# Block 2 attention: probabilities turned by VectorE and DMA instead of TensorE

## The chip, the core and the metric

The kernel runs on one core of one Trainium2 chip. The metric is device time in microseconds (us), the median over several executions. The engines are TensorE (PE; PEld is its weight load), VectorE (DVE), ScalarE (ACT), GpSimd (POOL) and SyncE (SP), whose queue issues nearly all DMAs.

## The reference, cut to what matters

Two blocks follow each other on a sequence of 512 rows of width 1024, in float32. Block 1 (windowed attention, a convolution, a gated feed-forward net) is not touched. Block 2 has two layers; each has 8 heads of chunked attention with a relative bias and 4 heads of retention. The part that the change touches is this attention:

```
scores = jnp.einsum("bnqhd,bnkhd->bnhqk", qc, kb) * (dh ** -0.5)
...
bias = rel_bias.astype(jnp.float32)[:, jnp.clip(dist, -REL_CLIP, REL_CLIP) + REL_CLIP]
...
scores = jnp.where(valid, scores + bias[None, None], NEG_INF)
p = jax.nn.softmax(scores, axis=-1)
out = jnp.einsum("bnhqk,bnkhd->bnqhd", p, vb)
...
y = jnp.concatenate([ya * jax.nn.silu(ag.astype(jnp.float32)),
                     yr * jax.nn.silu(rg.astype(jnp.float32))], axis=-1).astype(x.dtype)
return x + y @ w_out.astype(x.dtype)
```

A query in chunk c (64 rows) sees all keys of chunks 0 to c, its own chunk whole. The query rows are handled in four tiles i = 0 to 3 of 128 rows, and tile i needs 128(i+1) keys.

## The kernel before, in words

Each engine has its own queue, written out by hand in program order (class `Queues`, lines 174 to 217). An instruction waits for the names in its list and holds up whatever stands behind it on the same engine. `take` and `free` (303 to 310) guard buffers: who takes one waits for whoever freed it. Float32 products are made of a high and a low part: ScalarE rounds a tile to float32r (`wh` for weights), another engine subtracts to get the low part (`wl`), and TensorE does three matmuls (`mm3`), or two where one operand holds both parts. `prepare_to` (361) readies the weights three units ahead; the `wl` goes to GpSimd for the units in `POOL_LOW` (85), to VectorE for the rest. Each `wl` also releases the DMA of a later weight unit on SP.

Block 2 runs per layer through 26 steps, one for each entry of `SLOTS` (81): a projection of 24 matmuls of 512 columns, then `pieces_after` (1561), which puts the pieces of the attention between the projections. Each head's four query tiles come as two halves, tiles (3, 0) and (2, 1), 640 columns each, one half per step in steps 0 to 15. A half goes through this pipeline:

- Step s, `half_scores`: TensorE writes the scores into banks 4 and 5. `half_soft` (1402): VectorE adds the bias from the table tile `HK` and takes the row's extreme in one instruction (`m`, line 1417), does the same for the last 64 columns of the lower 64 rows (`M`, line 1421; the upper 64 rows of those columns hold a mask filled once by the loop at 1232), ScalarE takes the exponential with its row sum (`e`), VectorE the reciprocal of the sum (`r`, line 294), GpSimd multiplies the probabilities by it (`pn`, line 290), and a DMA copies the 640 columns to the tile `UA` (`pm`).
- Step s+2, `half_turn` (1447): TensorE turns the five 128x128 squares into banks 6 and 7 (line 249). `half_split` (1460): ScalarE rounds them to the high part (`ph`), VectorE subtracts (`pl`).
- Step s+3, for the second half, `head_values` (1479): 8 matmuls of values and turned probabilities into bank 3. `head_finish` (1499): ScalarE and VectorE add the two halves of the bank (`both_halves`, 877), GpSimd multiplies by the gate (`yg`), and the result is split for the output projection (`yh`, `yl`).

Within a step, TensorE's order is projection, values, turns, scores. Steps 16 to 25 hold the retention heads; they turn no probabilities, but their statistics go through small transposes on TensorE (`turn_squares`, `spread`) with a chain of short VectorE instructions (`head_rstd`, 530) between the two.

Of the kernel before, what the change touches and what calls it, by code (L numbers as in the profile page):

```python
# [28 lines left out]
MASKED = -1e30  # L29
# [20 lines left out]
XBH, XBL = Z + 22528, Z + 26624  # L50
PR = Z + 26368
R_COLS = Z + 30720


TP, TI = 0, 1280
T_COLS = TI + 128
# [13 lines left out]
TG0, TG1 = COS, Y + 5632  # L70
F_COLS = Y + 6760
X0H, X0L = Z + 16896, Z + 20992
# [11 lines left out]

POOL_LOW = {f"{l}{u}" for l in range(2) for u in ("q0", "v7", "k5", "q6", "q7", "k7", "g5", "g6", "g7")}

# [133 lines left out]
def two_blocks_kernel(nc, w_units, consts, dmat, x, x_rows, pvec, positions, rel, gain, out, stop=None):  # L220
# [6 lines left out]
    with ctx:  # L227
        RA = ctx.enter_context(nc.sbuf_tensor("RA", [128, R_COLS], F32R))
        FA = ctx.enter_context(nc.sbuf_tensor("FA", [128, F_COLS], F32))
        UA = ctx.enter_context(nc.sbuf_tensor("UA", [128, T_COLS], F32R))  # L230
        PS = [ctx.enter_context(nc.psum_tensor(f"ps{i}", [128, 512], F32)) for i in range(8)]
        Q = Queues()
# [998 lines left out]

        for i in range(4):
            G(f"fill.{i}", ["acl.21", "sin"], lambda e, i=i: e.memset(  # L1233
                F(SB + hoff[i] + 128 * i + 64, 64, 0, 64), -MASKED))

        zero("z2", K2P, 2048, ["gemm.br7"])

        for l in range(2):
# [89 lines left out]
            def evac_qk(i, w, b, key):  # L1328
# [73 lines left out]
            def half_soft(h, half):  # L1402
                pair = ((3, 0), (2, 1))[half]
                for n, i in enumerate(pair):
                    b = 4 + n
                    w = 128 * (i + 1)
                    pc = PB + hoff[i]
                    if h >= 8:
                        V(f"{pre}pn.{h}.{i}", [f"{pre}s.{h}.{i}", f"{pre}D.{h}"] + take(f"pb{i}"),
                          mul(F(pc, w), bank(b, w), F(DT + 512 * (h % 2), w)))  # L1410
                        free(f"bank{b}", f"{pre}pn.{h}.{i}")
                        continue
                    sc = SB + hoff[i]
# [6 lines left out]
                    V(f"{pre}M.{h}.{i}", [f"{pre}m.{h}.{i}"],  # L1420
                      lambda e, sc=sc, w=w, b=b, hk=hk, i=i: e.tensor_tensor_reduce(  # L1421
                          F(sc + w - 64, 64, 64, 128), bank(b, 64, w - 64, 64, 128),
                          steps(F(hk - w + 64, 1, 64, 128), [[-1, 64]]), -1.0, F(NM + i, 1, 64, 128),
                          ALU.add, ALU.min, F(NM + i, 1, 64, 128)))
                    free(f"bank{b}", f"{pre}M.{h}.{i}")
                    A(f"{pre}e.{h}.{i}", [f"{pre}M.{h}.{i}"] + take(f"pb{i}"), func(
                        F(pc, w), F(sc, w), ACT.Exp, scale=-1.0, bias=nm, accum=F(DE + i, 1)))
                    free(f"sb{i}", f"{pre}e.{h}.{i}")
                yield
                if h < 8:  # L1430
                    for i in pair:
                        V(f"{pre}r.{h}.{i}", [f"{pre}e.{h}.{i}"], recip(F(RD2 + i, 1), F(DE + i, 1)))
                    for i in pair:
                        w = 128 * (i + 1)
                        pc = PB + hoff[i]
# [3 lines left out]
                    for i in pair:  # L1439
                        free(f"pb{i}", f"{pre}pm.{h}.{half}")  # L1440
                if half == 1:
                    last = f"{pre}pn.{h}.1" if h >= 8 else f"{pre}M.{h}.1"
                    free(f"{'hk' if h < 8 else 'dt'}{h % 2}", last)
                    if h + 2 < 12:
                        load_head(h + 2)

            def half_turn(h, half):

                for n, i in enumerate(((3, 0), (2, 1))[half]):
                    if h >= 8:  # L1450
                        continue
                    b = 6 + n
                    for j in range(i + 1):
                        after = [f"{pre}pm.{h}.{half}"] + take(f"bank{b}") if j == 0 else []
                        T(f"{pre}pT.{h}.{i}" if j == i else None, after,
                          turn(bank(b, 128, 128 * j), U(TP + hoff[i] + 128 * j, 128)))
                if h < 8:
                    free(f"tp{half}", f"{pre}pT.{h}.{(0, 1)[half]}")

            def half_split(h, half):  # L1460
                parts = []
                for n, i in enumerate(((3, 0), (2, 1))[half]):
                    w = 128 * (i + 1)
                    if h < 8:
                        b = 6 + n
                        src = bank(b, w).rearrange("p (j q) -> p j q", j=i + 1)
                        d = lambda c, i=i: steps(R(c + 128 * i, 128), [[384, i + 1], [1, 128]])
                        parts.append((i, src, d(P2H), d(P2L), f"{pre}pT.{h}.{i}", f"bank{b}"))
# [30 lines left out]
            def head_finish(h):  # L1499
                if h < 8:  # L1500
                    yield from both_halves(f"{pre}yr.{h}", [f"{pre}o.{h}"] + (take("acc") if h % 2 == 0 else []), h % 2, ACC)
                    if h % 2:
                        p = h // 2
                        t, tn = t_slot()
                        G(f"{pre}yg.{p}", [f"{pre}yr.{h}", f"{pre}yr.{h - 1}", f"{pre}gt.{p}"] + take(tn),
                          mul(F(t), F(ACC), F(SG + 512 * (p % 2))))
                        free(f"sg{p % 2}", f"{pre}yg.{p}")
                        free("acc", f"{pre}yg.{p}")

                        def split():  # L1510
                            A(f"{pre}yh.{p}", [f"{pre}yg.{p}"], copy(R(YAH + 512 * p), F(t)))
                            G(f"{pre}yl.{p}", [f"{pre}yh.{p}"], sub(R(YAL + 512 * p), F(t), Rf(YAH + 512 * p)))
                            free(tn, f"{pre}yl.{p}")

                        later.append(split)
# [153 lines left out]
            xtm = [COS, SB, HK, DT]  # L1669
            xfree = [["1k7.l"], ["1e.7.1"], ["1M.7.1"], ["1pn.11.1"]]  # L1670

# [222 lines left out]
```

How the kernel before makes its waits and increments, by code:

```python
    def emit(self, engine, e, sems):  # L208
        waited = {}
        for name, waits, fn, sem, step in self.q[engine]:
            for s, v in waits:
                if waited.get(s, 0) < v:
                    e.wait_ge(sems[s], v)
                    waited[s] = v
            inst = fn(e)
            if name is not None:
                inst.then_inc(sems[sem], step)
# [343 lines left out]
                @block.sync  # L561
                def _(e):
                    Q.emit("sync", e, sems)
                    for s in sorted(Q.count):
                        if s.startswith("out") or stop:
                            e.wait_ge(sems[s], Q.count[s])
```

## Time and profile before

| | |
|---|---|
| median of 3 executions | 1206.74 us (1206.34 to 1206.87) |
| profiled execution, its own time | 1206.78 us |
| its span, first to last instruction | 1205.0 us |
| PE busy | 1196.4 us (99%) |
| DVE busy | 821.9 us (68%) |
| ACT busy | 553.9 us (46%) |
| POOL busy | 377.8 us (31%) |
| granted TensorE clock, mean | 0.998 of full speed |
| attention steps of layer 0 and of layer 1 | 705 to 820 us and 972 to 1087 us of the span |

Busy times come from one execution that the hardware profiler recorded. A matmul's recorded duration overlaps with its neighbours', so TensorE's cost is read from the distance between starts, or from the chain of work that ended last, where each piece counts once. Instructions that a helper issues bear the helper's line: 249 is every TensorE transpose of this kind, 297 every matmul, 274 every two-operand VectorE or GpSimd operation, 266 every ScalarE copy.

### The profile page before, as it was taken

To read this page: it belongs to the slowest core of one execution; us is meant where nothing else is said; L and a number is where in the kernel's file an instruction comes from. 1 tells how busy PE (TensorE), PEld (TensorE's weight loads), DVE (VectorE), ACT (ScalarE), POOL (GpSimd) and SP (SyncE) were. 2 spreads that over 40 slices of the span, in tenths; PEclk is the share of its full clock that TensorE was granted. 3 is DMA by queue.
4 is the path that set the end of the run, shared out by engine and by line. 5 is a ranking of instruction groups with operands and counts; after the bars stand their busy time and mean duration, and the time that the engine had idled before them with its cause. 6 is when DMAs were issued, how large, how long until landed. Compare 5 with 4: busy or idle time off the path is not lost.

```text
span 1205.0 us, 15117 instructions
## 1 busy us (share of the span) xinstructions
PE 1196.4 (99%) x5822; PEld 1008.1 (84%) x5822; DVE 821.9 (68%) x1530; ACT 553.9 (46%) x954; POOL 377.8 (31%) x277
## 2 busy tenths in 40 slices
PE   9999999999999999999999999999999999999997
PEld 7888888888888888888888889898888889898886
DVE  5878735466888536663568777777866866777875
ACT  6567533324444324332434465654334556654433
POOL 0135289997000000000000228775303033375200
PEclk9999999999999999999999999999999999999999
DMA  8233232323323322333223334433223334342251
GB/s 301 76 122 140 105 115 88 105 73 103 105 88 106 105 88 88 105 105 98 80 81 109 122 119 143 149 132 99 79 70 90 120 129 140 134 141 87 87 142 70
DMA packets 46744, 133.68 MB, mean 111 GB/s; under 512 B 4688, under 2 KB 10320, under 8 KB 46672
## 3 DMA queue, kind: packets, MB, share of 16 engines
q1 hardware_dynamic: 46240, 132.27, 33.8%
q8 instruction: 46, 0.75, 0.2%
q10 hardware_dynamic: 432, 0.44, 0.1%
q14 instruction: 26, 0.21, 0.1%
HBM read 114.35 MB, written 2.10 MB: 97 GB/s over the span
## 4 chain that ended last, share of the span: by engine, by line
PE 95%; DVE 2%; POOL 1%; ACT 1%; DMA 0%; issue 0%; ACTq 0%; POOLq 0%
PE ps L297 93%; PE ps L249 2%; DVE RA L274 1%; POOL FA L290 1%; DMA RA<-FA 0%; PE ps L551 0%; PE ps L492 0%; DVE FA L286 0%; ACT RA L266 0%; DVE FA L813 0%; DVE FA L274 0%; ACT FA L271 0%; ACT FA L270 0%; POOL RA L555 0%; DVE FA L1770 0%
## 5 line engine op out<-in xcount | busy, mean ns | idle before, releaser
L297 PE MATMUL ps<-RA 128*128 128x512 f32 (+1 forms) x5470 | 1177.8, 376 | 1.6 <-POOL RA L555 1.3
L297 PEld LDWEIGHTS ps<-RA 128*128 128x128 f32 x5470 | 974.5, 189 | 182.6 <-POOL RA L555 1.3
L266 ACT ACTIVATE RA<-FA 128x1024 fp32r<-128x1024 f32 (+5 forms) x338 | 280.2, 855 | 333.8 <-PE ps L297 167.2
L274 DVE TENSOR_TENSOR RA<-FA,RA 128x1024 fp32r<-128x1024 f32 (+6 forms) x303 | 321.8, 1073 | 162.8 <-ACT RA L266 161.1
L290 POOL TENSOR_SCALAR FA<-FA 128x256 f32<-128x256 f32 (+3 forms) x117 | 147.2, 1271 | 159.9 <-DVE FA L294 158.7
L286 DVE SCALAR_TENSOR_TENSOR FA<-ps,FA 128x512 f32<-128x512 f32 (+4 forms) x161 | 102.1, 638 | 90.8 <-PE ps L297 44.5
L274 POOL TENSOR_TENSOR FA<-FA 128x512 f32<-128x512 f32 (+1 forms) x82 | 108.3, 1322 | 88.1 <-ACT FA L270 66.7
L274 POOL TENSOR_TENSOR RA<-FA,RA 128x512 fp32r<-128x512 f32 (+1 forms) x37 | 69.7, 1893 | 109.5 <-ACT RA L266 109.5
L1233 POOL MEMSET FA<- 64x64 f32 x4 | 0.4, 145 | 328.7 <-ACT RA L266 328.7
L271 ACT ACTIVATE FA<-FA 128x512 f32<-128x512 f32 (+4 forms) x108 | 59.9, 555 | 90.3 <-DVE FA L1421 76.0
L270 ACT ACTIVATE FA<-ps,FA 128x512 f32<-128x512 f32 x56 | 38.1, 684 | 108.3 <-PE ps L297 108.3
L286 DVE SCALAR_TENSOR_TENSOR FA<-FA 128x512 f32<-128x512 f32 (+4 forms) x115 | 65.5, 578 | 16.3 <-ACT FA L266 8.0
L270 ACT ACTIVATE FA<-FA 128x512 f32<-128x512 f32 (+2 forms) x79 | 45.2, 576 | 64.9 <-DVE FA L286 45.0
L274 DVE TENSOR_TENSOR RA<-ps,RA 128x256 fp32r<-128x256 f32 (+3 forms) x109 | 53.4, 528 | 18.1 <-ACT RA L270 15.7
L274 DVE TENSOR_TENSOR FA<-ps,FA 128x512 f32<-128x512 f32 (+3 forms) x96 | 57.6, 619 | 5.8 <-PE ps L297 4.4
L286 DVE SCALAR_TENSOR_TENSOR RA<-FA,RA 128x512 fp32r<-128x512 f32 (+1 forms) x44 | 41.1, 941 | 19.8 <-ACT RA L270 19.0
L274 DVE TENSOR_TENSOR FA<-FA 128x512 f32<-128x512 f32 (+3 forms) x94 | 46.8, 499 | 6.6 <-ACT FA L270 4.0
L291 POOL TENSOR_SCALAR FA<-FA 128x512 f32<-128x512 f32 (+1 forms) x26 | 47.8, 1839 | 2.2
L270 ACT ACTIVATE RA<-FA 128x512 fp32r<-128x512 f32 (+1 forms) x50 | 35.0, 703 | 7.6 <-DVE FA L274 5.6
L266 ACT ACTIVATE RA<-ps 128x256 fp32r<-128x256 f32 (+2 forms) x95 | 37.3, 448 | 0.7
L270 ACT ACTIVATE FA<-ps 64x512 f32<-64x512 f32 (+1 forms) x48 | 28.3, 590 | 12.9 <-PE ps L297 12.0
L274 DVE TENSOR_TENSOR FA<-FA,ps 64x512 f32<-64x512 f32 (+1 forms) x32 | 21.8, 682 | 10.7 <-ACT FA L270 9.7
(51 smaller groups left out, 300.6 us busy)
## 6 DMA issues: line engine op xcount, KB each, us to landing
FA<-w_units SPq DMA_DIRECT2D x188, 512.0 KB, 3.5
UA<-FA SPq DMA_DIRECT2D x32, 320.0 KB, 2.5
RA<-FA SPq DMA_DIRECT2D x10, 512.0 KB, 3.2
FA<-rel SPq DMA_DIRECT2D x16, 256.0 KB, 3.7
FA<-w_units SPq DMA_DIRECT2D x8, 384.0 KB, 3.0
FA<-x SPq DMA_DIRECT2D x8, 256.0 KB, 6.0
FA<-x_rows SPq DMA_DIRECT2D x4, 512.0 KB, 9.4
FA<-dmat SPq DMA_DIRECT2D x8, 256.0 KB, 2.8
```

The costliest lines, as they stand in the source:

```text
L249: return lambda e: e.transpose(dst.bitcast(F32R), src, U(TI, 128))
L266: return lambda eng: eng.activation(dst, src, ACT.Copy)
L270: return lambda eng: eng.activation(dst, src, f, bias=bias, scale=scale)
L271: return lambda eng: eng.activation(dst, src, f, bias=bias, scale=scale, accum_out=accum)
L274: return lambda eng: eng.tensor_tensor(dst, a, b, op)
L286: return lambda eng: eng.scalar_tensor_tensor(dst, a, s, b, op0=op0, op1=op1)
L290: return lambda e: e.tensor_scalar(dst, src, s1, None, op0=op0)
L291: return lambda e: e.tensor_scalar(dst, src, s1, s2, op0=op0, op1=op1)
L297: return lambda e: e.matmul(dst, a, b, start=start, stop=stop_)
L1233: G(f"fill.{i}", ["acl.21", "sin"], lambda e, i=i: e.memset(F(SB + hoff[i] + 128 * i + 64, 64, 0, 64), -MASKED))
```

## The change

The reciprocal of the sum is no longer applied to the probabilities, but to the attention's output: the four reciprocals of a head go to HBM (`rs`), come back spread over 64 partitions (`rl`, into the tile `DB`), and GpSimd multiplies the gated output by them. The mask moves into the bias table: two memsets fill its upper left 64x64 corner once, the table is loaded by two DMAs for each head, and `m` covers all columns, so `M` goes. The probabilities are turned by one VectorE transpose in 32x32 squares (`vt`, into the tile `VT`), four DMAs that write its four groups of 32 partitions to HBM (`st`), and one DMA, issued a step later, that reads the turned half back (`ld`, into the tile `TPF`). `half_split` reads that tile in place of banks 6 and 7. `POOL_LOW` keeps two units per layer of nine; the low parts of rotated queries move from GpSimd to VectorE; in a step, `pl` comes behind the new half's `m` and `e`.

```diff
-POOL_LOW = {f"{l}{u}" for l in range(2) for u in ("q0", "v7", "k5", "q6", "q7", "k7", "g5", "g6", "g7")}
+POOL_LOW = {f"{l}{u}" for l in range(2) for u in ("g5", "g6")}
...
-        for i in range(4):
-            G(f"fill.{i}", ["acl.21", "sin"], lambda e, i=i: e.memset(
-                F(SB + hoff[i] + 128 * i + 64, 64, 0, 64), -MASKED))
+        for i in range(2):
+            G(f"fill.{i}", ["acl.21", "sin"], lambda e, i=i: e.memset(F(HK + 512 * i, 64, 0, 64), MASKED))
...
-                G(f"z.{k}", [f"f1q.{k}", f"0x.f{k}"], ts(hk, hk, F(PV + PV_GF + k, 1), ALU.mult))
+                G(f"z.{k}", [f"f1q.{k}", f"0x.f{k}", f"0vt.{(k + 2) // 2}.{k % 2}"], ts(hk, hk, F(PV + PV_GF + k, 1), ALU.mult))
...
-                (G if w == "q" else V)(f"{key}.l", [f"{key}.h"], sub(R(lo), F(t), Rf(h)))
+                V(f"{key}.l", [f"{key}.h"], sub(R(lo), F(t), Rf(h)))
...
-                    src = bass.AP(rel.tensor, rel.offset + (l * 8 + h) * 768 + 129, [[1, 128], [1, 512]])
-                    dma(f"{pre}hk.{h}", take(f"hk{h % 2}") + ["sin"], F(HK + 512 * (h % 2)), src, f"hk{h % 2}")
+                    at = rel.offset + (l * 8 + h) * 768 + 129 + 64
+                    dma(f"{pre}hk.{h}.0", take(f"hk{h % 2}") + ["sin"], F(HK + 512 * (h % 2) + 64, 448, 0, 64),
+                        bass.AP(rel.tensor, at, [[1, 64], [1, 448]]), f"hk{h % 2}")
+                    dma(f"{pre}hk.{h}", ["sin"], F(HK + 512 * (h % 2), 512, 64, 128),
+                        bass.AP(rel.tensor, at, [[1, 64], [1, 512]]), f"hk{h % 2}")
...
-                          F(sc, w - 64), bank(b, w - 64), steps(F(hk, 1), [[-1, w - 64]]), -1.0, 3.0e38,
-                          ALU.add, ALU.min, nm))
-                    V(f"{pre}M.{h}.{i}", [f"{pre}m.{h}.{i}"],
...
+                          F(sc, w), bank(b, w), steps(F(hk, 1), [[-1, w]]), -1.0, 3.0e38, ALU.add, ALU.min, nm))
...
-                    for i in pair:
-                        V(f"{pre}r.{h}.{i}", [f"{pre}e.{h}.{i}"], recip(F(RD2 + i, 1), F(DE + i, 1)))
...
-                        G(f"{pre}pn.{h}.{i}", [f"{pre}r.{h}.{i}"], ts(F(pc, w), F(pc, w), F(RD2 + i, 1), ALU.mult))
-                    dma(f"{pre}pm.{h}.{half}", [f"{pre}pn.{h}.{i}" for i in pair] + take(f"tp{half}"),
-                        U(TP + 640 * half, 640).bitcast(F32), F(PB + 640 * half, 640), f"pm{half}")
...
+                    half_store(h, half)
...
-            def half_turn(h, half):
...
-                          turn(bank(b, 128, 128 * j), U(TP + hoff[i] + 128 * j, 128)))
...
+            def half_store(h, half):
+                pair = ((3, 0), (2, 1))[half]
+                V(f"{pre}vt.{h}.{half}", [f"{pre}e.{h}.{i}" for i in pair] + take("vt"), lambda e: e.transpose(
+                    steps(F(VT, 1), [[32, 5], [160, 4], [1, 32]]), F(PB + 640 * half, 640).rearrange(
+                        "p (t c j) -> p t c j", t=5, c=4)))
...
+                for a in range(4):
+                    dma(f"{pre}st.{h}.{half}" if a == 3 else f"{pre}st.{h}.{half}.{a}",
+                        [f"{pre}vt.{h}.{half}"] + (take(f"turned{half}") if a == 0 else []),
+                        bass.AP(turned[half].tensor, turned[half].offset + 160 * a, [[640, 32], [20480, 4], [1, 160]]),
+                        steps(F(VT, 1, 32 * a, 32 * a + 32), [[160, 4], [1, 160]]), f"st{half}")
+                free("vt", f"{pre}st.{h}.{half}")
+                if half == 1:
+                    V(f"{pre}r.{h}", [f"{pre}e.{h}.{i}" for i in range(4)] + take("rd2"), recip(F(RD2, 4), F(DE, 4)))
+
+            def half_load(h, half):
+                dma(f"{pre}ld.{h}.{half}", [f"{pre}st.{h}.{half}"] + take(f"tp{half}"),
+                    TPF[0:128, 640 * half:640 * half + 640], turned[half], f"ld{half}")
+                free(f"turned{half}", f"{pre}ld.{h}.{half}")
+                if half == 1:
+                    Q.put("sync", f"{pre}rs.{h}", [f"{pre}r.{h}"] + take(f"rows{h % 2}"), lambda e: e.dma_start(
+                        bass.AP(rows[h % 2].tensor, rows[h % 2].offset, [[1, 128], [128, 4]]), F(RD2, 4),
+                        allow_slow_non_contiguous=True), "rs", 16)
...
+            def spread_rows(h):
+                p = 64 * (h % 2)
+                dma(f"{pre}rl.{h}", [f"{pre}rs.{h}", "gemm.0q0"] + (take("db") if h % 2 == 0 else []), Rf(DB, 512, p, p + 64),
+                    rows[h % 2].rearrange("(o n) -> o n", o=1).to_broadcast([64, 512]), "rl")
...
-                        G(f"{pre}yg.{p}", [f"{pre}yr.{h}", f"{pre}yr.{h - 1}", f"{pre}gt.{p}"] + take(tn),
-                          mul(F(t), F(ACC), F(SG + 512 * (p % 2))))
...
+                        G(f"{pre}ym.{p}", [f"{pre}yr.{h}", f"{pre}yr.{h - 1}", f"{pre}gt.{p}"],
+                          mul(F(ACC), F(ACC), F(SG + 512 * (p % 2))))
...
+                        G(f"{pre}yg.{p}", [f"{pre}ym.{p}", f"{pre}rl.{h}", f"{pre}rl.{h - 1}"], mul(F(ACC), F(ACC), Rf(DB)))
...
-                for c in fins + splits + fins + splits + soft:
-                    next(c, 0)
+                for h, half in loads:
+                    half_load(h, half)
+                for c in fins:
+                    next(c, 0)
+                for c in splits:
+                    next(c, 0)
+                for c in fins:
+                    next(c, 0)
+                for c in soft:
+                    next(c, 0)
+                for c in splits:
+                    next(c, 0)
```

## Rows read from the trace of the kernel before

**Rows 1.** The page: busy time, share of the span and instructions of each engine.

```profile
PE 1196.4 (99%) x5822; PEld 1008.1 (84%) x5822; DVE 821.9 (68%) x1530; ACT 553.9 (46%) x954; POOL 377.8 (31%) x277
```

**Rows 2.** The two longest waits of TensorE's matmuls, whole span: us in total, times, longest.

```profile
PE ps L297 <- POOL RA L555: 1.3, 1, 1.3
PE ps L249 <- DMA RA<-FA: 0.8, 2, 0.4
```

**Rows 3.** Chain that ended last, first, middle and last turns: start us, us, what.

```profile
712.16 0.39 PE ps L249 x5
...
741.15 0.42 PE ps L249 x5
...
1086.84 0.38 PE ps L249 x5
```

**Rows 4.** Timeline of TensorE, a step without turns, then one behind turns: start, us.

```profile
699.58 6.52 PE L297 MATMUL ps<-RA 128*128 128x512 f32 x29
...
705.71 6.45 PE L297 MATMUL ps<-RA 128*128 128x512 f32 x29
...
712.38 6.38 PE L297 MATMUL ps<-RA 128*128 128x512 f32 x28
718.60 0.29 PE L249 MATMUL ps<-UA 128*128 128x128 f32 x2
```

**Rows 5.** Busy time by stretch: attention and retention steps of both layers.

```profile
705.50:820.50 115.00, 115.00 (x681) 101.94 (x680) 81.93 (x235) 66.83 (x149) 81.18 (x60) 1.00 0.43 141
820.50:898.00 77.50, 77.50 (x388) 65.54 (x388) 60.82 (x131) 30.22 (x52) 22.04 (x12) 1.00 0.24 75
972.50:1087.50 115.00, 115.00 (x681) 101.92 (x681) 80.48 (x235) 66.53 (x148) 54.36 (x44) 1.00 0.42 138
1087.50:1165.00 77.50, 77.33 (x387) 64.96 (x386) 63.16 (x134) 31.72 (x55) 22.07 (x12) 1.00 0.29 89
```

The columns of rows 5 are length, then busy us and count of PE, PEld, DVE, ACT, POOL, then granted clock, DMA share, GB/s.

**Rows 6.** Groups by shape: count, busy us, mean ns, idle before.

```profile
L1421 DVE CUSTOM_DVE_ANT_0 FA<-ps,FA 64x64 f32<-64x64 f32 x64 | 18.6, 291 | 2.3
...
L294 DVE RECIPROCAL FA<-FA 128x1 f32<-128x1 f32 x68 | 10.7, 163 | 16.1 <-ACT FA L271 13.5 <-ACT FA L270 1.9
...
L1417 DVE CUSTOM_DVE_ANT_0 FA<-ps,FA 128x448 f32<-128x448 f32 x16 | 9.8, 613 | 0.0
...
L290 DVE TENSOR_SCALAR FA<-FA 128x512 f32<-128x512 f32 x2 | 1.0, 488 | 0.1
```

**Rows 7.** Timeline of one half scored before 734 us and turned at 748 us.

```profile
737.97 0.51 ACT L271 ACTIVATE FA<-FA 128x256 f32<-128x256 f32 x1
...
744.43 0.33 SPq L206 DMA_DIRECT2D FA<-w_units  x1
...
749.15 0.75 ACT L266 ACTIVATE RA<-ps 128x384 fp32r<-128x384 f32 x2
749.27 1.23 DVE L274 TENSOR_TENSOR RA<-FA,RA 128x1024 fp32r<-128x1024 f32 x1 [0.92 <-ACT RA L266]
750.53 0.89 DVE L274 TENSOR_TENSOR RA<-ps,RA 128x384 fp32r<-128x384 f32 x2
...
755.63 0.58 PE L249 MATMUL ps<-UA 128*128 128x128 f32 x5
...
755.98 1.29 POOL L274 TENSOR_TENSOR RA<-FA,RA 128x512 fp32r<-128x512 f32 x1
...
756.12 2.23 DVE L274 TENSOR_TENSOR RA<-FA,RA 128x1024 fp32r<-128x1024 f32 x1 [0.60 <-ACT RA L266]
```

**Rows 8.** DMA issues: count, KB each, median us from issue to landing.

```profile
UA<-FA SPq DMA_DIRECT2D x32, 320.0 KB, 2.5
RA<-FA SPq DMA_DIRECT2D x10, 512.0 KB, 3.2
...
out<-FA SPq DMA_DIRECT2D x7, 256.0 KB, 2.1
```

**Rows 9.** Timeline, TensorE at the end of layer 1's retention.

```profile
1151.58 3.54 PE L297 MATMUL ps<-RA 128*128 128x512 f32 x18 [0.17 <-DVE RA L274]
```

More of the change, by code:

```diff
@@ L51 @@
 PR = Z + 26368
+DB = Z + 29952
 R_COLS = Z + 30720
-TP, TI = 0, 1280
+TI = 0
 T_COLS = TI + 128
@@ L70 @@
 TG0, TG1 = COS, Y + 5632
-F_COLS = Y + 6760
+VT = Y + 6760
+F_COLS = VT + 640
 X0H, X0L = Z + 16896, Z + 20992
@@ L230, in two_blocks_kernel @@
         UA = ctx.enter_context(nc.sbuf_tensor("UA", [128, T_COLS], F32R))
+        TPF = ctx.enter_context(nc.sbuf_tensor("TPF", [128, 1280], F32))
+        turned = [nc.dram_tensor(f"turned{i}", (128, 640), F32, kind="Internal").ap() for i in range(2)]
+        rows = [nc.dram_tensor(f"rows{i}", (512,), F32, kind="Internal").ap() for i in range(2)]
         PS = [ctx.enter_context(nc.psum_tensor(f"ps{i}", [128, 512], F32)) for i in range(8)]
@@ L1415, in half_soft @@
                     hk = HK + 512 * (h % 2) + 127 + 128 * i
-                    V(f"{pre}m.{h}.{i}", [f"{pre}s.{h}.{i}", f"{pre}hk.{h}", "fill.3"] + take(f"sb{i}"),
+                    V(f"{pre}m.{h}.{i}", [f"{pre}s.{h}.{i}", f"{pre}hk.{h}", "fill.1"] + take(f"sb{i}"),
                       lambda e, sc=sc, w=w, b=b, hk=hk, nm=nm: e.tensor_tensor_reduce(
-                          F(sc, w - 64), bank(b, w - 64), steps(F(hk, 1), [[-1, w - 64]]), -1.0, 3.0e38,
-                          ALU.add, ALU.min, nm))
-                    V(f"{pre}M.{h}.{i}", [f"{pre}m.{h}.{i}"],
[L1421 to L1426, printed above, removed]
+                          F(sc, w), bank(b, w), steps(F(hk, 1), [[-1, w]]), -1.0, 3.0e38, ALU.add, ALU.min, nm))
+                    free(f"bank{b}", f"{pre}m.{h}.{i}")
+                    A(f"{pre}e.{h}.{i}", [f"{pre}m.{h}.{i}"] + take(f"pb{i}"), func(
                         F(pc, w), F(sc, w), ACT.Exp, scale=-1.0, bias=nm, accum=F(DE + i, 1)))
@@ L1430, in half_soft @@
                 if h < 8:
-                    for i in pair:
-                        V(f"{pre}r.{h}.{i}", [f"{pre}e.{h}.{i}"], recip(F(RD2 + i, 1), F(DE + i, 1)))
-                    for i in pair:
-                        w = 128 * (i + 1)
-                        pc = PB + hoff[i]
-                        G(f"{pre}pn.{h}.{i}", [f"{pre}r.{h}.{i}"], ts(F(pc, w), F(pc, w), F(RD2 + i, 1), ALU.mult))
-                    dma(f"{pre}pm.{h}.{half}", [f"{pre}pn.{h}.{i}" for i in pair] + take(f"tp{half}"),
-                        U(TP + 640 * half, 640).bitcast(F32), F(PB + 640 * half, 640), f"pm{half}")
-                    for i in pair:
-                        free(f"pb{i}", f"{pre}pm.{h}.{half}")
+                    half_store(h, half)
                 if half == 1:
-                    last = f"{pre}pn.{h}.1" if h >= 8 else f"{pre}M.{h}.1"
+                    last = f"{pre}pn.{h}.1" if h >= 8 else f"{pre}m.{h}.1"
                     free(f"{'hk' if h < 8 else 'dt'}{h % 2}", last)
@@ L1445, in half_soft @@
                         load_head(h + 2)
-            def half_turn(h, half):
[L1449 to L1455, printed above, removed]
-                          turn(bank(b, 128, 128 * j), U(TP + hoff[i] + 128 * j, 128)))
-                if h < 8:
-                    free(f"tp{half}", f"{pre}pT.{h}.{(0, 1)[half]}")
+            def half_store(h, half):
[3 more added lines that the diff above has]
+                        "p (t c j) -> p t c j", t=5, c=4)))
+                for i in pair:
+                    free(f"pb{i}", f"{pre}vt.{h}.{half}")
+                for a in range(4):
[6 more added lines that the diff above has]
+                    V(f"{pre}r.{h}", [f"{pre}e.{h}.{i}" for i in range(4)] + take("rd2"), recip(F(RD2, 4), F(DE, 4)))
@@ new lines, in half_load @@
+            def half_load(h, half):
[6 more added lines that the diff above has]
+                        allow_slow_non_contiguous=True), "rs", 16)
+                    free("rd2", f"{pre}rs.{h}")
@@ L1460, in half_split @@
+            def spread_rows(h):
+                p = 64 * (h % 2)
+                dma(f"{pre}rl.{h}", [f"{pre}rs.{h}", "gemm.0q0"] + (take("db") if h % 2 == 0 else []), Rf(DB, 512, p, p + 64),
+                    rows[h % 2].rearrange("(o n) -> o n", o=1).to_broadcast([64, 512]), "rl")
+                free(f"rows{h % 2}", f"{pre}rl.{h}")
             def half_split(h, half):
@@ L1464, in half_split @@
                     if h < 8:
[L1465 to L1468, printed above, removed]
+                        tile = (hoff[i] - 640 * half) // 128
+                        src = steps(TPF[0:128, 640 * half + 32 * tile:640 * half + 32 * tile + 1],
+                                    [[32, i + 1], [160, 4], [1, 32]])
+                        d = lambda c, i=i: steps(R(c + 128 * i, 128), [[384, i + 1], [32, 4], [1, 32]])
+                        parts.append((i, src, d(P2H), d(P2L), f"{pre}ld.{h}.{half}", None))
                     else:
@@ L1476, in half_split @@
                     V(f"{pre}pl.{h}.{i}", [f"{pre}ph.{h}.{i}"], sub(dl, src, dh.bitcast(F32)))
-                    free(where, f"{pre}pl.{h}.{i}")
+                    if where:
+                        free(where, f"{pre}pl.{h}.{i}")
+                if h < 8:
+                    free(f"tp{half}", *[f"{pre}pl.{h}.{i}" for i in ((3, 0), (2, 1))[half]])
             def head_values(h):
@@ L1503, in head_finish @@
                         p = h // 2
[L1504 to L1508 removed]
+                        G(f"{pre}ym.{p}", [f"{pre}yr.{h}", f"{pre}yr.{h - 1}", f"{pre}gt.{p}"],
+                          mul(F(ACC), F(ACC), F(SG + 512 * (p % 2))))
+                        free(f"sg{p % 2}", f"{pre}ym.{p}")
+                        G(f"{pre}yg.{p}", [f"{pre}ym.{p}", f"{pre}rl.{h}", f"{pre}rl.{h - 1}"], mul(F(ACC), F(ACC), Rf(DB)))
+                        free("db", f"{pre}yg.{p}")
                         def split():
[L1511 to L1513 removed]
+                            A(f"{pre}yh.{p}", [f"{pre}yg.{p}"], copy(R(YAH + 512 * p), F(ACC)))
+                            G(f"{pre}yl.{p}", [f"{pre}yh.{p}"], sub(R(YAL + 512 * p), F(ACC), Rf(YAH + 512 * p)))
+                            free("acc", f"{pre}yl.{p}")
                         later.append(split)
@@ L1565, in pieces_after @@
                 turns = lag(2, False) + lag(1, True)
+                loads = lag(1, False)
                 news = scores_at.get(s, [])
@@ L1568, in pieces_after @@
                     head_values(h)
-                for h, half in turns:
-                    half_turn(h, half)
+                    if h < 8:
+                        spread_rows(h)
                 for h, half in news:
@@ L1669, in two_blocks_kernel @@
             xtm = [COS, SB, HK, DT]
[L1670 removed]
+            xfree = [["1k7.l"], ["1e.7.1"], ["1m.7.1"], ["1pn.11.1"]]
             hm = [K2P, K2P + 1024, RVH, RVH + 1024]
```

## The prediction, made before the result was known

> **What bounds the kernel now.** I read the page first: TensorE is busy for 1196.4 us, 99% of the span, and VectorE, the next, for 68% [rows 1]. A busy TensorE need not be a tight one, so I read its waits next: the longest is 1.3 us in all, the next 0.8 [rows 2]. TensorE waits for nobody worth the name, and the chain that ended last runs through it nearly from start to end. The reader should see there that the turns of Block 2 stand in the chain as pieces of their own: 32 groups of five, the first at 712.16 us and the last at 1086.84, each 0.38 to 0.43 us [rows 3]. So time goes down with TensorE's work, as long as the work that takes its place stays within the lag that the pipeline allows. The stretches by stage say how much room the others have there: in the 115 us of either layer's attention VectorE is busy for 80 to 82 us and ScalarE for 67; in the 77.5 us of retention behind it VectorE is busy for 60.8 and 63.2 [rows 5]. VectorE is where room could run out.
>
> **The change part by part.** The sum is made against the profiled execution's own 1206.78 us (1.8 us of it lie around the span of 1205.0); it stands 0.04 us above the median of 1206.74, which is nothing.
>
> TensorE. All 160 turns go. The pieces of the 32 groups in the chain add up to 12.8 us (half of them about 0.38, half about 0.42 [rows 3]). There is a little more: two starts that bracket 28 matmuls in a step without turns are 705.71 - 699.58 = 6.13 us apart [rows 4]; the same 28 widths behind a group of turns take 718.60 - 712.38 = 6.22 us [rows 4]. So the matmuls behind a group start 0.09 us late. The bounds are 0 and 32 x 0.09 = 2.9 us. In half of the steps the narrow matmuls of the values stand before the scores and may slow them as well, so I take half, 1.5 us. TensorE's gain is 14.3 us.
>
> VectorE in an attention layer (16 halves, 32 tiles). Out go 32 `M` at 0.29 = 9.3 us and 32 reciprocals at 0.163 = 5.2 us; back come 8 reciprocals, 1.3 us [rows 6]. Each `m` gets 64 columns more; from the rows for 448 and 64 columns, (613 - 291) / 384 = 0.84 ns a column, that is 0.054 us x 32 = 1.7 us [rows 6]. Two weight low parts (`v7`, `k5`) come over from GpSimd at 1.23 us = 2.5 us [rows 7], and the low part of `q4`, half as wide, 0.6. New are 16 transposes `vt` of 640 columns, which no row shows. From below: the 512-column operation with one source takes 488 ns, so 0.61 us for 640 [rows 6]. From above: an instruction of one column costs 0.163 us [rows 6]; if each of the 20 column blocks of 32 cost as much as that, 3.3 us. It is one instruction with one source, so it is nearest to the streaming rows; at the pace of `m` it takes 613 + 192 x 0.84 = 774 ns, which I take: 12.4 us. The net is 4.0 us on 81.9, so 86 of the 108 us that the stage then has. No stall follows from that.
>
> The Trainium skill ("Vector Engine (DVE) Microarchitecture Reference", section 3.8) says that the transposing front end is pipelined for one element per cycle and lane; with the 0.96 GHz of its page "VectorE: DVE Perf Modes" that gives an estimate of 0.67 us, and VectorE's sum would be 1.7 us lower per layer. No run here shows it yet.
>
> VectorE in a retention stretch. Four weight low parts (4 x 1.23) and three low parts of rotated queries (about half as wide, 3 x 0.6) come over: 6.7 us, giving 67.5 and 69.9 us busy of 77.5. Something comes back: an operation with two SBUF inputs that takes 1.23 us alone took 2.23 us where it started beside a GpSimd operation [rows 7], and GpSimd loses 7 of its 12 operations there [rows 5]. But one matmul already waits for VectorE at 1151.58, for 0.17 us [rows 9]. I add 0.5 us for this and like places; bounds 0 and 8 us (below, as a rival).
>
> The round trip. Take the half whose last exponential ends at 737.97 + 0.51 = 738.5 us [rows 7]. It will end a little earlier (`pl` now stands behind it on VectorE, `M` is gone), but `vt` comes after `pl` (0.89 us [rows 7]) and takes 0.8, so it ends near 739. Four stores go out one behind the other; a store to HBM lands 2.1 us after its issue, the old copy in 2.5, larger copies of this kind in 3.2 [rows 8]. With half a us per issue the last lands near 743.5; bounds 742 and 745. The load `ld` stands on SP behind the weight load issued at 744.43 [rows 7], so it goes out at about 744.8, and with the old copy's 2.5 us, or 3.5 behind a weight load, the data are there at 747.3 to 748.3. ScalarE wants them for `ph` at 749.15 [rows 7]: nothing waits. TensorE wants the low part later still: the values of that half end at 755.63 and take about 1.2 us, so from 754.4; `ph` and `pl` need 0.75 + 0.89, so TensorE waits only if the load lands after 752.7, some 4 us late. Cost: nothing, covered by two projections of 24 matmuls.
>
> `VT` is one buffer, so the next `vt` waits for the stores: 0.8 + 2 + 2.5 = 5.3 us against a step of 6.8 us. Behind a late `vt` on VectorE would stand the next evacuation and the next weight low part; those are three units ahead.
>
> SP issues 14 DMAs a head in place of 3. At half a us that is 7 us of the 13.5 us of two steps. Queued behind a waiting `st` or `ld` are weight loads, which are wanted three steps later. The store `rs` writes 512 single elements, which no row resembles; between the 2.1 us of a store and several times that it is covered, since `rl` needs it two steps later. GpSimd loses 32 `pn` per layer and gains four products: less load. The mask costs two memsets where four were, and a second DMA of the table per head, which starts a head ahead. Cost of all this: nothing; if the cover failed, it would be the round trip's price.
>
> Sum: 1206.78 - 12.8 - 1.5 + 0.5 = 1193.0 us.
>
> **The rivals.**
>
> *A, as forecast*: 1193.0 us, own range 1191.4 (the whole 2.9 us behind the turns, no new wait) to 1196. For it: TensorE's empty list of waits and VectorE's room [rows 2, 5]. Chance 0.68.
>
> *B, the round trip overruns.* Write receipts from HBM, four stores in a row, a load behind a weight load: if the half lands more than 4 us later than I reckon, TensorE waits once for each head, 16 times. It costs 16 us for each us beyond the margin; 0.9 us beyond it eats the gain, 1 us gives 1193 + 16 = 1209 us, slower than before. Against it: the margin is more than a whole landing of any kind shown [rows 8]. Chance 0.10.
>
> The Trainium skill speaks for B and against the change: "VectorE: DVE Perf Modes", section "Rules for kernel authors", says to turn 128x128 on TensorE if PSUM will do as the destination, and VectorE only within 32x32. Its page "DMA: Bandwidth & Descriptors" puts about 2 us of fixed cost on a DMA and most of that on the write's receipt, longest from HBM; the trace agrees with landings of 2.1 to 2.5 us [rows 8].
>
> *C, VectorE becomes the bound in attention.* At 3.3 us a transpose, 16 x 3.3 - 8.4 = 44 us are added to 81.9: 126 us for 108 us of TensorE, 18 us lost in each layer, 1229 us. It begins to bind at (108 - 73.5) / 16 = 2.2 us a transpose and decides at 2.6. Chance 0.08.
>
> *D, VectorE is late in retention.* The statistics of each retention head go TensorE, VectorE, TensorE; with VectorE at 90% each may come 1 us late. Eight heads: 8 us, 1201 us, still faster. For it: the wait at 1151.58 [rows 9] and the 6.7 us added. Against it: VectorE's gaps there and fewer operations of GpSimd beside it. Chance 0.12.
>
> Something near no change by a mixture: 0.02.
>
> **How the numbers follow.** The likeliest is A, 1193.0 us. A and D together hold 0.80, so the range goes from 1191.4 to 1202.5. A measurement of this kernel can tell about 0.2% (2.4 us) from no change. Faster: A and D, and a little of B where it overruns by less than 0.7 us, 0.82. Slower: the rest of B and C, 0.15. Within 0.2%: 0.03.
>
> **What would show it.** Right: no group of L249 from 712 to 1087 us, the two attention stretches 7 us shorter each, no wait of TensorE there for VectorE or ScalarE, transposes near 0.8 us, loads landed before `ph` starts. B would show as TensorE waiting for VectorE's `pl`, and ScalarE before it for a DMA into `TPF`, once a head. C would show as transposes above 2 us and VectorE near 100% of the attention stretches. D would show as waits of TensorE at the retention transposes (lines 492 and 551) for VectorE's chain of short instructions. Waits on `VT` would show as VectorE waiting for a DMA before each transpose. The prediction would be wrong above all if an HBM store or load takes some 4 us more than the rows of before say.

## The result, and the profile after

The changed kernel takes 1270.15 us (1267.92 to 1272.0), the kernel before beside it 1206.54 us: a ratio of 1.0527 [1.0513, 1.054]. I had forecast 1193.0 us and a gain. The profiled execution has a span of 1267.2 us, 62.2 more than before. The page of the changed kernel, busy time first, then 40 slices of the span:

```profile
PE 1210.0 (95%) x5662; PEld 1014.0 (80%) x5662; DVE 839.3 (66%) x1408; ACT 555.1 (44%) x954; POOL 269.0 (21%) x197
...
PEclk9999999999999999999999998889999988889999
DMA  7243323222233322232233787863223488773251
```

TensorE's 160 turns are gone (5662 instructions where 5822 were [rows 1]), yet its busy time is 13.6 us longer, and it stands idle for 57 us of the span, against 8.6 before [rows 1]. The slices with the lower granted clock are all in attention, where the DMA digits stand at 6 to 8. The waits that matter, in us in total, times, longest:

```profile
PE ps L302 <- DVE RA L279: 43.7, 19, 5.6
PE ps L302 <- DVE FA L1424: 3.3, 3, 1.7
...
ACT RA L271 <- DMA TPF<-turned: 100.3, 24, 8.5
DVE FA L1444 <- DMA turned<-FA: 29.6, 10, 6.1
```

Where TensorE waited for nobody [rows 2], it now waits for VectorE's low parts. For 36.7 of these 43.7 us, in 12 waits, they are those of the probabilities (`pl`); `pl` waits for ScalarE's `ph`, and `ph` for the loads into `TPF`. The timeline of two heads shows what is late (start, us, engine, what, the idle time before it):

```profile
734.08 0.58 SPq L208 DMA_DIRECT2D TPF<-turned  x1
734.71 0.44 SPq L1463 DMA_DIRECT2D rows<-FA  x1
735.27 1.89 SPq L208 DMA_DIRECT2D turned<-FA  x4
...
742.79 0.83 ACT L271 ACTIVATE RA<-TPF 128x384 fp32r<-128x384 f32 x2 [6.38 <-DMA TPF<-turned]
743.35 0.90 DVE L279 TENSOR_TENSOR RA<-TPF,RA 128x384 fp32r<-128x384 f32 x2 [3.26 <-ACT RA L271]
...
744.30 7.99 PE L302 MATMUL ps<-RA 128*128 128x512 f32 x60 [0.69 <-DVE RA L279]
...
747.56 0.34 SPq L208 DMA_DIRECT2D TPF<-turned  x1
747.66 0.84 DVE L1444 STREAM_TRANSPOSE FA<-FA 128x640 f32<-128x640 f32 x1 [3.42 <-DMA turned<-FA]
...
753.25 0.43 SPq L1463 DMA_DIRECT2D rows<-FA  x1
...
762.95 0.83 ACT L271 ACTIVATE RA<-TPF 128x384 fp32r<-128x384 f32 x2 [8.18 <-DMA TPF<-turned]
...
764.55 0.77 PE L302 MATMUL ps<-RA 128*128 128x512 f32 x1 [5.60 <-DVE RA L279]
```

The load issued at 734.08 us is in use only at 742.79, 8.7 us later; the median landing of these loads is 4.0 us. The stores issued from 735.27 hold back VectorE's next transpose, which waits for its buffer until 747.66, and SyncE, whose load of them goes out at 747.56. SyncE stands so for 97.3 us in 15 times, and whatever is queued behind the load stands with it. All of this stands around the issue of `rs` at 734.71 (line 1463), the store of a head's 512 reciprocals as single elements, and it repeats at the next `rs`, 753.25. The loads without an `rs` beside them are quick: the one of 747.56 is in use at 750.19. The DMA share and rate of 730 to 752 us, in 40 slices of 0.55 us:

```profile
DMA  8778623967989999949198995938924202977851
GB/s 251 279 194 215 175 74 139 184 104 261 320 347 332 285 175 273 191 12 53 22 69 65 103 78 44 91 47 172 112 52 127 75 0 56 289 297 194 211 146 75
```

From 739.4 us on (slice 18) there are slices nine tenths busy at 53 to 112 GB/s; three of that share between 735.5 and 737.7 us moved 285 to 332. The DMA engines are busy there, and move little.

### The profile page after: what moved, and what is told of

Same layout as the page of the kernel before. It is cut to its first block and busy times, and to the rows that moved or that the text cites. A ratio compares the mean times of both kernels' runs of the same rounds, so it can differ in the third digit from the quotient of the medians.

```text
span 1267.2 us, 14787 instructions
## 1 busy us (share of the span) xinstructions
PE 1210.0 (95%) x5662; PEld 1014.0 (80%) x5662; DVE 839.3 (66%) x1408; ACT 555.1 (44%) x954; POOL 269.0 (21%) x197
## 5 line engine op out<-in xcount | busy, mean ns | idle before, releaser
L302 PE MATMUL ps<-RA 128*128 128x512 f32 (+1 forms) x5470 | 1199.0, 381 | 50.7 <-DVE RA L279 43.7
L302 PEld LDWEIGHTS ps<-RA 128*128 128x128 f32 x5470 | 994.0, 193 | 241.1 <-DVE RA L279 49.3
L279 DVE TENSOR_TENSOR RA<-FA,RA 128x1024 fp32r<-128x1024 f32 (+4 forms) x325 | 337.5, 1049 | 163.7 <-ACT RA L271 162.0
L295 POOL TENSOR_SCALAR FA<-FA 128x256 f32<-128x256 f32 (+2 forms) x53 | 73.3, 1394 | 112.6 <-DVE FA L299 64.9
L271 ACT ACTIVATE RA<-TPF 128x512 fp32r<-128x512 f32 (+1 forms) x64 | 26.5, 462 | 100.4 <-DMA TPF<-turned 100.3
L279 DVE TENSOR_TENSOR RA<-TPF,RA 128x512 fp32r<-128x512 f32 (+1 forms) x64 | 32.8, 552 | 51.9 <-ACT RA L271 51.9
L1444 DVE STREAM_TRANSPOSE FA<-FA 128x640 f32<-128x640 f32 x32 | 27.0, 844 | 37.3 <-DMA turned<-FA 29.6
L279 POOL TENSOR_TENSOR RA<-FA,RA 128x512 fp32r<-128x512 f32 (+1 forms) x15 | 23.7, 1587 | 105.7 <-ACT RA L271 105.7
L275 ACT ACTIVATE FA<-ps 64x512 f32<-64x512 f32 (+1 forms) x48 | 28.4, 593 | 16.9 <-PE ps L302 13.2
```

The costliest lines, as they stand in the source:

```text
L271: return lambda eng: eng.activation(dst, src, ACT.Copy)
L275: return lambda eng: eng.activation(dst, src, f, bias=bias, scale=scale)
L279: return lambda eng: eng.tensor_tensor(dst, a, b, op)
L295: return lambda e: e.tensor_scalar(dst, src, s1, None, op0=op0)
L302: return lambda e: e.matmul(dst, a, b, start=start, stop=stop_)
L1444: V(f"{pre}vt.{h}.{half}", [f"{pre}e.{h}.{i}" for i in pair] + take("vt"), lambda e: e.transpose(steps(F(VT, 1), [[32, 5], [160, 4], [1, 3 ...
```

## The experiments

Three theories stood at the start. **T1**: the element store `rs` holds up the transfers beside it. **T2**: the broadcast load `rl`, which puts the row of reciprocals on 64 partitions, does. **T3**: the round trip of the probabilities through HBM is too slow by itself. The first runs each alter one part of the change.

**Runs of 16 bytes.** `rs` writes the same 2 KB as 128 runs of 16 bytes, so the reciprocals come to stand in another order.

```diff
-    bass.AP(rows[h % 2].tensor, rows[h % 2].offset, [[1, 128], [128, 4]]), F(RD2, 4),
+    bass.AP(rows[h % 2].tensor, rows[h % 2].offset, [[4, 128], [1, 4]]), F(RD2, 4),
```

> One part changed: the store of the four reciprocals of a head (rs) writes the same 2 KB to HBM as 128 runs of 16 bytes instead of 512 single elements of 4 bytes, so the sums land in another order and the division is by wrong rows. Theory 1 (the 512 element writes hold up the DMAs around them): a quarter of the writes, the hold-up falls from about 10 us to 2 or 3, mostly covered: 1193 to 1205 us. Theory 2 (the broadcast load rl, 64 reads of the same 2 KB, holds them up): 1265 to 1272 us. Theory 3 (the way through HBM is too slow in itself, four stores and a load): 1265 to 1272 us.

One run: 1191.79 us, 1.2 us below the range that T1 gave and far from the other two. TensorE's longest wait is again the 1.3 us that it had before [rows 2]; the longest landing of a `TPF` load falls from 12.0 to 6.0 us:

```profile
ACT RA L271 <- DMA TPF<-turned: 10.7, 12, 2.1
PE ps L302 <- DVE RA L279: 0.7, 3, 0.3
```

The same bytes to the same 2 KB, in runs of 16, cost nothing that can be seen; as single elements they cost the whole loss. T1 holds. T3 falls, since the whole round trip is still there, and T2 has little left, since `rl` is there as well.

**Without the broadcast load.** The output is multiplied by ones.

```diff
-    dma(f"{pre}rl.{h}", [f"{pre}rs.{h}", "gemm.0q0"] + ..., Rf(DB, 512, p, p + 64), rows[h % 2]...to_broadcast([64, 512]), "rl")
+    G("ones", ["gemm.0q0"], lambda e: e.memset(Rf(DB), 1.0))
```

> The broadcast load rl is left out; the output is multiplied by a tile of ones, so the division by the sums is left out; the element store rs stays as it is. Theory 1 (element store): 1255 to 1272 us, loads into TPF still landing up to 10 us after their issue. Theory 2 (broadcast load): 1193 to 1200 us. Theory 3 (HBM round trip itself): 1255 to 1272 us.

One run: 1258.19 us. TensorE still waits 36.2 us in 14 times for VectorE's low parts (19.3 us of it, in 8 times, for `pl`), and the slowest `TPF` load takes 12.1 us. T2 explains at most the 12 us by which this is below the changed kernel; it is not the cause.

**The reciprocals turned first.** VectorE turns the reciprocals too, in a tile of 32 columns, and four DMAs store them as 16 runs of 128 bytes.

```diff
-    V(f"{pre}r.{h}", ..., recip(F(RD2, 4), F(DE, 4)))
+    V(f"{pre}r.{h}", ..., recip(F(RW, 4), F(DE, 4)))
+    V(f"{pre}rt.{h}", [f"{pre}r.{h}"] + take("rd2"), lambda e: e.transpose(F(RW + 32, 32), F(RW, 32)))
...
-    Q.put("sync", f"{pre}rs.{h}", ..., [[1, 128], [128, 4]]), F(RD2, 4), ...
+    for a in range(4):
+        dma(..., bass.AP(rows[h % 2].tensor, rows[h % 2].offset + 32 * a, [[128, 4], [1, 32]]),
+            F(RW + 32, 32, 32 * a, 32 * a + 4), "rs")
```

> Nothing left out: the four reciprocals are turned by one more VectorE transpose of 32 columns (0.2 us a head) and stored as 16 runs of 128 bytes by four DMAs, in the order that rl reads. Theory 1: the hold-up goes, TensorE waits for nothing in the attention: 1192 to 1197 us, about 1% below the kernel before. Theories 2 and 3: 1262 to 1272 us.

1192.71 us (1191.99 to 1192.99), 0.9885 [0.9869, 0.9902] of before: faster than both kernels. Its page, its list of TensorE's waits and its attention stretches with the retention behind the second (columns as in rows 5):

```profile
PE 1181.6 (99%) x5662; PEld 993.7 (83%) x5662; DVE 835.7 (70%) x1424; ACT 555.6 (47%) x954; POOL 265.5 (22%) x198
```

```profile
PE ps L303 <- POOL RA L561: 1.3, 1, 1.3
PE ps L303 <- DVE RA L280: 0.7, 3, 0.3
PE ps L255 <- DMA RA<-FA: 0.7, 2, 0.4
```

```profile
705.50:813.50 108.00, 108.00 (x601) 94.75 (x600) 92.69 (x180) 66.05 (x146) 39.75 (x27) 1.00 0.69 203
...
972.50:1080.00 107.50, 107.50 (x601) 94.76 (x600) 88.14 (x179) 64.33 (x141) 14.32 (x11) 1.00 0.67 197
1080.00:1157.50 77.50, 77.06 (x393) 64.76 (x392) 65.72 (x137) 32.88 (x54) 11.34 (x7) 1.00 0.37 111
```

TensorE does in 108.0 and 107.5 us, without a gap and at the full clock, the 601 matmuls that are left of the 681 in 115 us [rows 5] when 80 turns go.

**The sums on the probabilities, as before.** No `rs`, no `rl`; the rest of the change stays.

```diff
+    for i in pair:
+        V(f"{pre}r.{h}.{i}", [f"{pre}e.{h}.{i}"], recip(F(RD2 + i, 1), F(DE + i, 1)))
+    for i in pair:
+        G(f"{pre}pn.{h}.{i}", [f"{pre}r.{h}.{i}"], ts(F(pc, w), F(pc, w), F(RD2 + i, 1), ALU.mult))
-    V(f"{pre}vt.{h}.{half}", [f"{pre}e.{h}.{i}" for i in pair] + take("vt"), ...
+    V(f"{pre}vt.{h}.{half}", [f"{pre}pn.{h}.{i}" for i in pair] + take("vt"), ...
```

> The sums are applied to the probabilities on GpSimd as before, so neither rs nor rl exists; the turn by VectorE and HBM, the mask in the table and the moved low parts stay. Nothing is left out. Theories 1 and 2: the round trip is 2 us longer by pn, still covered: 1193 to 1198 us. Theory 3: 1240 to 1272 us.

1233.37 us (1233.1 to 1233.97), 1.0222 [1.0207, 1.0238]: a miss for all theories. The waits show a stall of another kind:

```profile
DVE FA L1449 <- POOL FA L294: 71.7, 32, 3.3
...
ACT RA L270 <- DMA TPF<-turned: 20.7, 14, 2.9
```

The DMAs are in time (20.7 us of ScalarE's waits, where the changed kernel had 100.3). VectorE stands before each of its 32 transposes for GpSimd's products, and all that is queued behind the transpose stands with it. Of TensorE's waits only 2.8 us, in 2 times, are for the `pl` that a late load would delay.

**The products on VectorE.** To try that reading, the run before with one letter changed.

```diff
-    G(f"{pre}pn.{h}.{i}", [f"{pre}r.{h}.{i}"], ts(F(pc, w), F(pc, w), F(RD2 + i, 1), ALU.mult))
+    V(f"{pre}pn.{h}.{i}", [f"{pre}r.{h}.{i}"], ts(F(pc, w), F(pc, w), F(RD2 + i, 1), ALU.mult))
```

> The run with the sums applied to the probabilities took 1233.4 us, and there VectorE stood 71.7 us before its transposes, waiting for GpSimd's products. Here VectorE makes these products itself; all else as there (no row of sums goes through HBM, nothing is left out). If that wait is the cause, 1192 to 1202 us, though VectorE has some 25 us more to do. If the later start of the round trip is the cause, whoever makes the products, 1215 to 1235 us.

1194.25 us (1193.94 to 1194.63), 0.9901 [0.9885, 0.9918]. The wait for GpSimd was the cause. The stretch of layer 0's attention in this run:

```profile
705.50:820.50 115.00, 114.60 (x630) 100.08 (x629) 104.76 (x233) 69.42 (x151) 36.51 (x24) 1.00 0.65 189
```

VectorE is busy for 104.8 of 115 us there, and still TensorE waits for its low parts only 1.3 us in the whole run: more work on VectorE cost next to nothing, 2.2 us of waiting in its queue (71.7 us in 32 times) cost some 39 us (1233.4 against 1194.3). The intervals of this run and of the turned store overlap, so which of the two is faster stays open.

**The sums on the output alone.** The kernel before, with `rs`, `rl` and the products on the output, and nothing else of the change: TensorE keeps its turns and the copy inside SBUF in front of them.

```diff
-    dma(f"{pre}pm.{h}.{half}", [f"{pre}pn.{h}.{i}" for i in pair] ...
+    dma(f"{pre}pm.{h}.{half}", [f"{pre}e.{h}.{i}" for i in pair] ...
+    rows_store(h); spread_rows(h)   # rs and rl as in the change
```

> The kernel before with one part of the change alone: the sums applied to the output, by the element store and the broadcast load; TensorE keeps its turns, and the probabilities reach them by a copy inside SBUF. T1: that copy runs beside the element store, and the copy and the weight reads are held up as in the changed kernel, though with no round trip through HBM: 1215 to 1260 us. T3 (the round trip is too slow by itself, the element store only tips it): the copy has the slack, 1203 to 1212 us.

1223.63 us (1222.24 to 1225.6), 1.0143 [1.0128, 1.0158], within T1's range. Its DMA issues (KB each, median us to landing):

```profile
UA<-FA SPq DMA_DIRECT2D x32, 320.0 KB, 6.5
...
rows<-FA SPq DMA_DIRECT2D x16, 2.0 KB, 9.6
```

The copy from SBUF to SBUF, which touches no HBM, lands in 6.5 us where it took 2.5 [rows 8], and TensorE waits 8.6 us in 5 times for it. A round trip through HBM is not needed for a loss. With it the loss is larger; in the round trip two transfers for each half, one behind the other, can be held up where here it is one, but that this is the whole difference was not tried.

**An extra element store, nobody waiting.** The kernel with the turned store gets, behind it, a DMA of zeros to an unused place, which nothing reads; six variants differ in that place, one of them also in the number of elements. This one is the old pattern of `rs`:

```diff
+    Q.put("sync", f"{pre}xs.{h}", [f"{pre}r.{h}", "xs0"] + take("spare"), lambda e: e.dma_start(
+        bass.AP(spare.tensor, spare.offset, [[1, 128], [128, 4]]), F(RD2, 4),
+        allow_slow_non_contiguous=True), "xs", 16)
```

> This is the kernel with the turned store (1192.7 us) plus, behind that store on SyncE, a second one of 512 single 4-byte elements to an unused place in HBM, which nothing reads and no computation waits for. T1 (the element store holds up the transfers beside it): most of the loss comes back, 1245 to 1272 us, and the TPF loads land late again, up to 12 us. Rival (the loss needs somebody who waits for the element store, the broadcast load and GpSimd behind it): within 3 us of 1192.7.

1273.92 us (1270.11 to 1274.64), 1.056 [1.0543, 1.0578]: the whole loss is back, 1.9 us more than T1's range allowed, though no computation depends on the store. The same waits are back with it:

```profile
ACT RA L273 <- DMA TPF<-turned: 98.4, 25, 9.4
PE ps L304 <- DVE RA L281: 45.1, 17, 6.8
```

SyncE does not wait for the extra store either; it waits 99.9 us in 14 times for stores into `turned` to land, where without the extra store it waited 6.8 us in 9 times. The other places:

```diff
- [[1, 128], [128, 4]]), F(RD2, 4)
+ [[128, 128], [16384, 4]]), F(RD2, 4)      # 512 bytes apart
```

> As the run with 512 extra elements, but the elements lie 512 bytes apart in HBM. If the loss comes from many writes to the same few places in HBM, which wait for each other, it goes away: 1191 to 1200 us. If the number of elements counts, wherever they lie, 1245 to 1272 us, the same as when they lie side by side.

```diff
- bass.AP(spare.tensor, spare.offset, [[1, 128], [128, 4]]), F(RD2, 4)
+ steps(F(RX, 1), [[2, 4]]), F(RD2, 4)      # to SBUF
```

> As the run with 512 extra elements, but the elements go to an unused place in SBUF (128 partitions, 4 elements each, 8 bytes apart) instead of HBM. If single elements cost the DMA rings as such, 1245 to 1272 us. If it is the write of a part of a line in HBM, 1191 to 1200 us.

```diff
- [[1, 128], [128, 4]]), F(RD2, 4)
+ [[1, 128], [1, 1]]), F(RD2, 1)            # 128 elements side by side
```

> As the run with 512 extra elements side by side, but with 128 of them: one 4-byte element of each partition, 512 bytes of HBM in all. If the cost goes with the number of writes that fall into one place, about a quarter of the 512, so some 2 us of stall in place of 8, which the slack covers: 1192 to 1215 us. If any set of neighbouring 4-byte writes is enough, 1245 to 1272 us.

```diff
- [[1, 128], [128, 4]]), F(RD2, 4)
+ [[16, 128], [2048, 4]]), F(RD2, 4)        # 64 bytes apart
```

> As the run with 512 extra elements, which lie 64 bytes apart in HBM (512 bytes apart the time was 1193.3 us, side by side 1273.9 us). If writes disturb each other only within one piece of 64 bytes or less, 1191 to 1196 us; if the piece is larger (256 or 512 bytes), 1200 to 1272 us.

```diff
- [[1, 128], [128, 4]]), F(RD2, 4)
+ [[4, 128], [512, 4]]), F(RD2, 4)          # 16 bytes apart
```

> As the run before, with the 512 elements 16 bytes apart. If the piece within which writes disturb each other is 32 or 64 bytes, some of the loss comes back: 1195 to 1250 us. If only the same 16 bytes matter, 1191 to 1196 us.

| The extra store, once a head | us | its median landing, us |
|---|---|---|
| none (the turned store alone) | 1192.7 | |
| 512 x 4 bytes, to SBUF | 1192.9 | 3.3 |
| 512 x 4 bytes, HBM, 512 bytes apart | 1193.3 | 3.8 |
| 512 x 4 bytes, HBM, 64 bytes apart | 1193.5 | 3.7 |
| 512 x 4 bytes, HBM, 16 bytes apart | 1196.6 | 4.4 |
| 128 x 4 bytes, HBM, side by side | 1256.7 | 9.2 |
| 512 x 4 bytes, HBM, side by side | 1273.9 | not in the trace |

The rows behind two of these landings, 128 elements side by side and then 512 elements 512 bytes apart:

```profile
spare<-FA SPq DMA_DIRECT2D x16, 0.5 KB, 9.2
```

```profile
spare<-FA SPq DMA_DIRECT2D x16, 2.0 KB, 3.8
```

The number of elements and their size do not decide by themselves, and a target in SBUF costs nothing: what costs is that single 4-byte elements lie side by side in HBM. A quarter of the elements took most of the loss (64 of 81 us), against the expectation that the cost goes with their number; `rs` itself, four times the elements, lands in 9.6 us where these 128 take 9.2. The path differs there: the `TPF` loads land within 5.9 us, and it is the stores of the turned halves that are late, up to 9.2 us, so that VectorE stands before its transposes:

```profile
DVE FA L1448 <- DMA turned<-FA: 64.2, 13, 6.6
```

At 16 bytes apart the 3.9 us over the turned store alone are not clear of the noise (two runs; 0.9919 [0.99, 0.9939] against 0.9885 [0.9869, 0.9902]), so which half of that expectation held stays open.

## Why the prediction was wrong

**The step that failed** is the sentence on `rs`: "between the 2.1 us of a store and several times that it is covered, since `rl` needs it two steps later". I bounded the time of `rs` itself and asked only who waits for it. Nobody on the path does: GpSimd waits 27.6 us for `rl`, and TensorE not once for GpSimd there. What I left out is what it does to the DMAs beside it. The run with the extra store shows that this alone brings the whole loss, and the stores in runs of 16 and of 128 bytes show that without it the forecast comes out. I had no row like it and priced it at nothing all the same, though the diff shows how the bytes lie: 512 elements, each an address of its own, in 2 KB of HBM.

The cover of `VT` went with it: I set 5.3 us for a transpose and its stores against a step of 6.8 us, but the stores issued from 735.27 us held the buffer until 747.66, and VectorE stood 29.6 us in 10 times for it.

**How the stall became 62 us.** TensorE's margin for the loads was some 4 us in my working, and a load beside `rs` came up to 8 us late, so what I had as rival B took place, with another cause: neither receipts nor the row of four stores, which in the run with the turned store land in 2.1 us as forecast. Against that run the span of the changed kernel is 77.0 us longer, the 62.2 us of the result and 14.8 us of gain that were lost. TensorE stands still for 1267.2 - 1210.0 = 57.2 us in place of 8.6, which gives 48.6; the same 5662 matmuls are busy for 1210.0 in place of 1181.6 us, which gives 28.4. Rival B's price had only the first. The second goes with the granted clock, 0.975 of full speed in the mean where the run with the turned store has 1.000: an estimate from these, 1181.6 / 0.975 = 1211.9 us, is close to the 1210.0. Stretches of the changed kernel (columns as in rows 5):

```profile
705.50:820.50 115.00, 94.88 (x480) 81.46 (x479) 70.71 (x138) 55.77 (x123) 35.51 (x23) 0.92 0.81 151
820.50:898.00 77.50, 74.37 (x360) 63.48 (x360) 61.52 (x122) 32.37 (x62) 16.74 (x11) 0.92 0.45 113
...
764.55:768.00 3.45, 3.45 (x12) 3.06 (x12) 2.44 (x7) 2.94 (x9) 1.45 (x2) 0.52 0.58 188
768.00:772.00 4.00, 4.00 (x20) 3.31 (x19) 4.00 (x8) 3.12 (x8) 3.92 (x2) 1.00 0.78 142
```

Behind the wait of 5.60 us the granted clock is 0.52, nearly all of the stretch at 1.2 GHz in place of 2.4. The matmuls of 512 columns there are recorded with 682 ns in the mean (4 of them), those of the next stretch, at 1.00, with 405 ns (18).

**What was right**, read from the run with the turned store. TensorE: 7.0 and 7.5 us shorter in the two attention stretches, 14.5 against the 14.3 that I summed; its whole busy time and the span are both 14.8 shorter, with the same 8.6 us idle. The transpose, taken at 774 ns, bounds 0.61 and 3.3 us:

```profile
L1446 DVE STREAM_TRANSPOSE FA<-FA 128x640 f32<-128x640 f32 x32 | 27.0, 844 | 8.4 <-ACT FA L277 8.3
```

844 ns, so rival C is out. The estimate of 0.67 us from the Trainium skill ("Vector Engine (DVE) Microarchitecture Reference", section 3.8) was too low by a fifth. VectorE has 92.7 and 88.1 us in the attention stretches where I had 86; 1.7 us of each is the added turn of the reciprocals. The largest rest in the first stretch is the low parts of 1024 columns, 16 at 1556 ns where before there were 13 at 1373. Rival D did not come: TensorE waits for VectorE's low parts 0.7 us in 3 times, all of them in the retention stretches, against 0.3 us in 2 times before, so the 0.5 us that I added for it was about right. The lower bound of rival A was mis-summed: 1206.78 - 12.8 - 2.9 is 1191.1, not 1191.4, and nothing hangs on it. The round trip: stores 2.1 us as taken, loads 4.2 where I took 2.5 to 3.5, so ScalarE does wait for them, 9.9 us in 11 times; the margin hides all of it from TensorE. The rule of the Trainium skill that I had set against the change ("VectorE: DVE Perf Modes", "Rules for kernel authors": a 128x128 turn belongs on TensorE if PSUM will do) loses here: the change with the turned store takes 1.15% less time than the kernel before (the ratio 0.9885). With TensorE busy for 99% of the span [rows 1] the slower way around it is the cheaper one.

**Applying the sums to the output** I costed as load taken off GpSimd. Its worth is another: with the products on GpSimd, VectorE's transposes wait 71.7 us and the kernel takes 1233.4 us. But it was not the only way out, as the products on VectorE show.

## What to carry to other kernels

Price a DMA by how its bytes lie on the far side and by what runs beside it, not only by who waits for it; a transfer that no row resembles needs a bound for what it does to its neighbours too. Turn a column of numbers into a row on an engine first, and let the DMA store runs of 16 bytes or more. When an operation moves to another engine's queue, ask what stands still behind it there: VectorE had room for 64 more products (27 us, 280 to 594 ns each) and none for 32 waits of 2.2 us.

## What the runs showed of the hardware

Stores of 4-byte elements side by side in HBM slow the core's other DMAs beside them. The loads into `TPF` take up to 12.0 us where the median is 4.0; copies inside SBUF take 6.5 us in place of 2.5; and the three weight reads of 512 KB issued from 730 to 752 us take 5.4 us (median) in the changed kernel and 3.8 in the run with the turned store. 128 such elements (512 bytes) take 7.4 to 9.8 us to land, 512 elements spread by 64 bytes 3.7 us. Of the two cheap patterns nearest to it, 4 bytes every 16 bytes is at most some 4 us longer in the whole kernel, and full runs of 16 bytes side by side show no cost (1191.8 us, one run). Both put four writes into each 64 bytes, the costly pattern sixteen; that the writes to one small piece of HBM wait for each other would fit all these runs, but none shows what happens inside. The Trainium skill ("DMA: Bandwidth & Descriptors", "Specifications") says that a transfer below 512 bytes makes the engine read, modify and write. By that alone the runs of 16 bytes and the elements 512 bytes apart should have been slow as well; here they cost nothing that can be seen (1191.8 and 1193.3 us against 1192.7).
